# Expert loop of a two-layer encoder trunk: eight trips of one expert become four trips of two, and one selection matrix of 256 columns gathers the rows of both

## The reference

```
logits = (h @ w_router).astype(jnp.float32) + b_router.astype(jnp.float32)
top_val, top_idx = lax.top_k(logits, TOP_K_EXPERTS)
top_w = jax.nn.softmax(top_val, axis=-1)
gates = jnp.sum(jax.nn.one_hot(top_idx, N_EXPERTS, dtype=jnp.float32) * top_w[..., None], axis=-2)
for e in range(N_EXPERTS):
    out = out + gates[..., e:e + 1] * swiglu(h, w_gu[e], w_down[e])
```

## Time and profile before

| | us |
|---|---|
| median of three runs | 1984.95 |
| the profiled execution | 1984.88 |
| its span | 1983.1 |
| PE busy (share of the span) | 1940.6 (98%) |
| DVE busy | 1545.9 (78%) |
| ACT busy | 1278.7 (64%) |
| mean granted TensorE clock | 0.995 of full |
| HBM read | 510.53 MB |

### The profile page before, as it was taken

The page is one execution under the profiler, slowest core; times in us unless marked ns, Lnnn a source line. Parts: engine busy times, 40 slices in busy tenths (PEclk is TensorE's granted clock), DMA queues, the critical chain, the costliest instruction groups (busy, mean ns, idle before and its releaser), DMA issues.

```text
span 1983.1 us, 28233 instructions
## 1 busy us (share of the span) xinstructions
PE 1940.6 (98%) x9436; PEld 1610.3 (81%) x9436; DVE 1545.9 (78%) x1754; ACT 1278.7 (64%) x1698; POOL 58.2 (3%) x83
## 2 busy tenths in 40 slices
PE   8999999999999999999899999999999999999997
PEld 6887788888888887788788888888888888888886
DVE  4887665555456887664698998989989899898996
ACT  4647544544445647544577787777877778777785
POOL 1020000000000010001000000000000000000000
PEclk9999999999999999999999999999999999999998
DMA  8453554555554454553499999999999999999993
GB/s 269 137 189 109 194 206 139 169 192 198 182 191 132 128 173 149 193 197 110 148 362 352 354 377 346 353 350 352 379 354 347 348 351 380 349 352 350 355 375 149
DMA packets 178005, 512.52 MB, mean 258 GB/s; under 512 B 8225, under 2 KB 17377, under 8 KB 177938
## 3 DMA queue, kind: packets, MB, share of 16 engines
q1 hardware_dynamic: 175266, 502.47, 70.2%
q0 software_dynamic: 2544, 9.09, 1.5%
q10 hardware_dynamic: 128, 0.08, 0.0%
HBM read 510.53 MB, written 1.07 MB: 258 GB/s over the span
## 4 chain that ended last, share of the span: by engine, by line
PE 84%; DVE 7%; issue 4%; ACT 3%; POOL 1%; DMA 1%; DVEq 0%; SPq 0%; ACTq 0%; POOLq 0%
PE bank L867 14%; PE bank L862 14%; PE bank L863 14%; PE bank L1679 7%; PE bank L1685 7%; PE bank L1693 7%; PE bank L660 4%; PE bank L673 4%; PE bank L669 4%; DVE wlo L487 3%; PE bank L1706 2%; PE bank L812 2%; PE bank L906 1%; ACT whi L484 1%; PE bank L1977 1%
## 5 line engine op out<-in xcount | busy, mean ns | idle before, releaser
L487 DVE TENSOR_TENSOR wlo<-raw,whi 128x1024 fp32r<-128x1024 f32 (+3 forms) x958 | 1130.6, 1218 | 185.7 <-ACT whi L484 155.7
L484 ACT ACTIVATE whi<-raw 128x1024 fp32r<-128x1024 f32 (+3 forms) x958 | 995.2, 1057 | 281.7 <-PE bank L867 156.5
L862 PE MATMUL bank<-whi,xg_hi 128*128 128x512 f32 x896 | 351.8, 393 | 1.7 <-ACT whi L484 1.7
L863 PE MATMUL bank<-whi,xg_lo 128*128 128x512 f32 x896 | 348.9, 389 | 0.0
L867 PE MATMUL bank<-wlo,xg_hi 128*128 128x512 f32 x896 | 277.1, 390 | 3.1 <-DVE wlo L487 3.1
L867 PEld LDWEIGHTS bank<-wlo,xg_hi 128*128 128x128 f32 x896 | 167.4, 188 | 41.7 <-DVE wlo L487 7.1
L862 PEld LDWEIGHTS bank<-whi,xg_hi 128*128 128x128 f32 x896 | 168.2, 188 | 36.1 <-ACT whi L484 2.1
L863 PEld LDWEIGHTS bank<-whi,xg_lo 128*128 128x128 f32 x896 | 168.3, 188 | 34.0
L862 PE MATMUL bank<-whi,hidTw_hi 128*128 128x512 f32 x448 | 175.8, 392 | 0.0
L863 PE MATMUL bank<-whi,hidTw_lo 128*128 128x512 f32 x448 | 174.4, 389 | 0.0
L1679 PE MATMUL bank<-whi,hT_hi 128*128 128x512 f32 (+3 forms) x576 | 152.5, 388 | 6.0 <-ACT hT_hi L1375 5.1
(11 more groups left out here) (317 smaller groups left out, 2029.5 us busy)
## 6 DMA issues: line engine op xcount, KB each, us to landing
raw<-in_moe_w_gu SPq DMA_DIRECT2D x224, 1024.0 KB, 6.9
raw<-in_moe_w_down SPq DMA_DIRECT2D x112, 1024.0 KB, 7.3
raw<-in_w_in SPq DMA_DIRECT2D x34, 1024.0 KB, 5.1
raw<-in_ffn_w_gu SPq DMA_DIRECT2D x28, 1024.0 KB, 5.2
raw<-in_xa_wkv SPq DMA_DIRECT2D x16, 1024.0 KB, 5.0
raw<-in_ffn_w_down SPq DMA_DIRECT2D x14, 1024.0 KB, 4.9
raw<-in_w_branch SPq DMA_DIRECT2D x12, 1024.0 KB, 5.0
raw<-in_w_out SPq DMA_DIRECT2D x8, 1024.0 KB, 5.0
```

The costliest lines, as they stand in the source:

```text
L484: self.eng.activation(whi[:, ps, 0:size], src, ACT.Copy).then_inc(high_ready, mark(high_ready, "high", p))
L487: self.eng.tensor_tensor(wlo[:, ps, 0:size], src, whi[:, ps, 0:size].bitcast(F32), ALU.subtract).then_inc(low_ready, mark(low_ready, "low" ...
L862: pe.matmul(bank[b][:, :], hi[:, k], wh, start=first, stop=False)
L863: pe.matmul(bank[b][:, :], lo[:, k], wh, start=False, stop=False)
```

## The change

The loop has four trips of two experts. `find` fills `pick` with 256 columns, 128 for either expert; the gather for the next two experts stands in the second half of a trip, in two parts. `h` itself is kept split: ACT makes `h_hi`, DVE `h_lo`, both float32r, so the gather is a float32r product, with `pick` in float32r. It takes the high halves first and the low halves after. The body of a trip holds both experts' code, and the queues of ACT, DVE and SP have twice the length too. Core of the diff:

```diff
-            "experts": (1, segments[1][0], segments[1][1], E, 0),
+            "experts": (1, segments[1][0], segments[1][1], E // 2, 0),
...
-        def gather_pe(pe, g, which):
+        GATHER = ((1, 3), (0, 2))
+
+        def gather_pe(pe, g, which, part):
 
             pe.wait_ge(expert_step, at(g, "pick", which))
-            if which == "first":
-                pe.wait_ge(norm_ready, at(1, "ffn", "normed", 1))
-            for half in range(2):
-                b = GATHER[half]
+            for t in range(NT):
+                pe.wait_ge(high_copied, at("h_hi", t))
+            for b in GATHER[part]:
                 fill(pe, b, "dve")
-                for i in range(4):
-                    for t in range(NT):
-                        ins = pe.matmul(bank[b][:, i * P:(i + 1) * P], h[:, t, (4 * half + i) * P:(4 * half + i + 1) * P],
-                                        pick[:, t], start=t == 0, stop=t == NT - 1)
-                ins.then_inc(bank_full[b], mark(bank_full[b], g, "gather", which, half))
+            for low in range(2):
+                for t in range(NT):
+                    if low:
+                        pe.wait_ge(norm_ready, at("h_lo", t))
+                    for n_, b in enumerate(GATHER[part]):
+                        for i in range(2):
+                            k = 4 * part + 2 * n_ + i
+                            src = h_lo[:, t] if low else h_hi[t]
+                            ins = pe.matmul(bank[b][:, i * 2 * P:(i + 1) * 2 * P], src[:, k * P:(k + 1) * P], pick[:, t, :],
+                                            start=not low and t == 0 and i == 0, stop=bool(low) and t == NT - 1 and i == 1)
+                        if low and t == NT - 1:
+                            ins.then_inc(bank_full[b], mark(bank_full[b], g, "gather", which, part, n_))
...
             with tally.trips(pe, g, trips):
                 q = [0]
...
+                for hf in range(2):
+                    e = f"{g}.{hf}"
+                    mine = slice(hf * P, hf * P + P)
...
+                        if j == N - 1:
+                            if hf:
+                                gather_pe(pe, g, "next", 0)
+                            down(j - 1, last=2)
+                            turn_hidden(j)
+                            if hf:
+                                gather_pe(pe, g, "next", 1)
+                            down(j - 1, first=2)
...
                 for t in range(NT):
-                    dve.tensor_scalar(pick[:, t], iota, cur[:, t:t + 1], None, ALU.is_equal).then_inc(
-                        expert_step, mark(expert_step, g, "pick", which))
+                    for hf in range(2):
+                        dve.tensor_scalar(pick[:, t, hf * P:(hf + 1) * P], iota, cur[:, hf, t:t + 1], None, ALU.is_equal).then_inc(
+                            expert_step, mark(expert_step, g, "pick", which))
...
+                expert(f"{g}.0", gate_back, False)
+                expert(f"{g}.1", cur[:, 0, 2:4], True)
...
+        def split_h(dve, t):
+            dve.wait_ge(high_copied, at("h_hi", t))
+            dve.scalar_tensor_tensor(h_lo[:, t, :], h[:, t, :], rstd(1, "ffn", t), h_hi[t][:, :].bitcast(F32), ALU.mult,
+                                     ALU.subtract).then_inc(norm_ready, mark(norm_ready, "h_lo", t))
...
+                    act.wait_ge(rstd_ready, at(l, "ffn", "rstd"))
+                    high_of_h(0)
                     act.wait_ge(bank_full[0], at("router"))
                     act.activation(logits_T[:, :], bank[0][0:E, 0:S], ACT.Copy).then_inc(
                         act_freed[0], mark(act_freed[0], "logits_out"))
+                    high_of_h(1)
...
                     dve.wait_ge(rstd_ready, at(l, "ffn", "rstd"))
-                    for t in range(NT):
-                        dve.tensor_scalar(h[:, t, :], h[:, t, :], rstd(l, "ffn", t), None, ALU.mult).then_inc(
-                            norm_ready, mark(norm_ready, l, "ffn", "normed", t))
+                    split_h(dve, 0)
                 if l:
                     route(dve)
-                    mixer_dve(dve, sp_, "experts", lambda: route_again(dve))
+                    mixer_dve(dve, sp_, "experts", lambda: (split_h(dve, 1), route_again(dve)))
```

More of the change, by code:

```diff
@@ L824, in back_pe @@
+        def gathered_pe(pe, g, which):
+            for part in range(2):
+                for n_, b in enumerate(GATHER[part]):
+                    pe.wait_ge(dve_freed[b], at("lo", g, "gather", which, part, n_))
+        def back_pe(pe, e, which, t):
+            pe.wait_ge(dve_freed[4], at(e, "y", 0, which))
+            pe.wait_ge(dve_freed[5], at(e, "y", 1, which))
             for nb in range(2):
@@ L841, in mixer_pe @@
             l, u0, p0, trips, rnd = MIXERS[g]
-            gather_pe(pe, g, "first")
+            for part in range(2):
+                gather_pe(pe, g, "first", part)
             fill(pe, 4, "dve")
@@ L852, in mixer_pe @@
                 q = [0]
[L854 to L882, removed]
-                        else:
-                            parts = [(per * i + c, b0, per * i + c == 0, per * i + c == KD - 1) for c in range(per)]
-                        piece((xg_hi, xg_lo), parts, False)
-                    same(g, name, j)
@@ L888, in down @@
[L888 to L899, removed]
@@ L939, in mixer_act, with high_gathered, take_y @@
             l, u0, p0, trips, rnd = MIXERS[g]
[L941 to L947, removed]
+            def high_gathered(which, part):
+                for n_, b in enumerate(GATHER[part]):
+                    act.wait_ge(bank_full[b], at(g, "gather", which, part, n_))
+                    k = 4 * part + 2 * n_
+                    act.activation(xg_hi[:, k:k + 2], heads(bank[b][:, :], 2),
+                                   ACT.Copy).then_inc(high_copied, mark(high_copied, "hi", g, "gather", which, part, n_))
+            def take_y(e, which, full):
                 for nb in range(2):
@@ L950, in take_y @@
                     act.activation(y_hi[:, 512 * nb:512 * nb + 512], bank[4 + nb][:, :], ACT.Copy).then_inc(
-                        y_high, mark(y_high, g, "y high", nb, which))
-            high_gathered("first")
+                        y_high, mark(y_high, e, "y high", nb, which))
+            for part in range(2):
+                high_gathered("first", part)
             act.wait_ge(bank_full[4], at(g, "empty", 0))
@@ L1001, in mixer_dve, with find @@
+                expert(f"{g}.0", lambda step: previous(f"{g}.1", step), False)
+                expert(f"{g}.1", lambda step: at(f"{g}.0", step), True)
+            take_y(g, "last", [(bank_full[4], final(f"{g}.1", "out0")), (piece_used, final(f"{g}.1", "out1"))])
         def mixer_dve(dve, sp_, g, meanwhile=lambda: None):
             l, u0, p0, trips, rnd = MIXERS[g]
-            def find(which, row):
+            def find(which, rows):
                 if which == "first":
@@ L1008, in find @@
                 else:
[L1009 removed]
+                    dve.tensor_copy(gate_back[:, :], cur[:, 1, 2:4]).then_inc(expert_step, mark(expert_step, g, "gate back", which))
                 dve.wait_ge(expert_step, at(g, "gate back", which))
[L1011 removed]
+                dve.tensor_copy(cur[:, :, :], rows).then_inc(expert_step, mark(expert_step, g, "cur", which))
                 dve.wait_ge(expert_step, at(g, "cur", which))
@@ L1014, in find @@
                 for t in range(NT):
-                    dve.tensor_scalar(pick[:, t], iota, cur[:, t:t + 1], None, ALU.is_equal).then_inc(
-                        expert_step, mark(expert_step, g, "pick", which))
-            def low_gathered(which):
-                for half in range(2):
-                    dve.wait_ge(high_copied, at("hi", g, "gather", which, half))
-                    b = GATHER[half]
-                    dve.tensor_tensor(xg_lo[:, 4 * half:4 * half + 4], heads(bank[b][:, :], 4), xg_hi[:, 4 * half:4 * half + 4].bitcast(F32),
-                                      ALU.subtract).then_inc(dve_freed[b], mark(dve_freed[b], "lo", g, "gather", which, half))
@@ L1025, in take_y, with low_gathered @@
-            def take_y(which):
+                    for hf in range(2):
+                        dve.tensor_scalar(pick[:, t, hf * P:(hf + 1) * P], iota, cur[:, hf, t:t + 1], None, ALU.is_equal).then_inc(
+                            expert_step, mark(expert_step, g, "pick", which))
+            def low_gathered(which, part):
+                for n_, b in enumerate(GATHER[part]):
+                    dve.wait_ge(high_copied, at("hi", g, "gather", which, part, n_))
+                    k = 4 * part + 2 * n_
+                    dve.tensor_tensor(xg_lo[:, k:k + 2], heads(bank[b][:, :], 2), xg_hi[:, k:k + 2].bitcast(F32),
+                                      ALU.subtract).then_inc(dve_freed[b], mark(dve_freed[b], "lo", g, "gather", which, part, n_))
@@ L1040, in mixer_dve @@
-            find("first", tab[:, rnd, 0:1, :])
```

(26 more changed lines are left out.)

282 lines of the change are left out of this document (180 added, 102 removed).

## The result

The changed kernel takes 1993.14 us (median of five, 1991.42 to 1995.33) against 1984.95 us (1983.18 to 1985.75): a ratio of 1.0042, interval 1.0031 to 1.0053, so 8.2 us slower. The forecast was 1983.4. The profiled execution took 1995.33 us with a span of 1993.5.

What follows compares the result with a forecast made beforehand. The prediction took the expert loop to be bound by PE, with DVE next. Its terms, -13.3 - 0.6 + 1.0 + 7.2 + 4.2 = -1.5 us, gave 1983.4 us from 1984.88, range 1971.5 to 1989.5.

Steps and rivals of the forecast that it cites:

- Gathers: Expert loop: four float32r gathers of 3.81 us replace eight float32 ones of 3.57 us on PE; 13.3 us less.
- `find`: PE's wait behind DVE's `find` in the expert loop: four longer ones instead of eight; 0.6 us less.
- Ahead of the loop: Before the expert loop: splitting `h`, two more selections and a longer first gather add 1.0 us, bounds 0 and 2.
- so I take 2.4, between 1.9 and the full 3.4: PE's idle gap at each of three backward branches, the doubled body being fetched again; +7.2 us, bounds 0 and 10.1.
- The sequencer's net lead: At the loop's branch: 2.4 us ahead less about 0.9 of waits, hiding 1.5 of the extra 3.37 us.
- The clock: Half clock on PE behind the three branches: half of 2.8 us taken for each, +4.2 us, bounds 0 and 8.5.
- the clock falls at every branch: Rival at the edges between trips: full 3.4 us gaps and 2.8 us for each clock fall; 1990.6 us, chance 0.16.
- The first rival: The doubled loop body stays loaded, so PE's backward branches cost no refetch; 1972.0 us, chance 0.25.

Runs made afterwards that it cites:

- after_no_loop: The changed kernel with the four trips of its expert loop written out on PE, ACT, DVE and SP, so no branch goes back; 1969.72 us, ratio 0.9927.

## Why the prediction was wrong

**Gathers: right.** The last trip's two parts take 1.91 and 1.99 us, 3.90 against 3.81, 0.119 us for each matmul, as read from the earlier trace rows. From the loop's first matmul to its last piece's first, the trips written out take 974.34 us (976.86 to 1951.20) after the change and 988.13 (976.24 to 1964.37) before it: 13.8 less, against 13.9 forecast with `find`.

**`find`: right.** PE's wait behind it, against the earlier trace rows, four times instead of eight:

```profile
1126.74 0.39 PE L877 MATMUL bank<-whi,xg_lo 128*128 128x512 f32 x1
1127.88 0.73 PE L881 MATMUL bank<-wlo,xg_hi 128*128 128x512 f32 x2 [0.75 <-DVE wlo L489]
```

**Ahead of the loop: right for what it counted.** The loop's first matmul is 1.15 us later (978.30, before 977.15); forecast +1.0. Uncounted was the half clock from 978.31 to 981.72, 1.7 us, which the other kernels (above) show as a chance of this execution, not a cost of the change. The half-clock stretch ahead of it, which in both kernels covers the first gather, was not the last one this time.

**The step that failed: "so I take 2.4, between 1.9 and the full 3.4".** That the body would be fetched anew at each of three edges was right, and PE's branch does make the gap. The size was wrong, and beyond its upper bound: 15.1 us against 7.2, bound 10.1. I took the branch's length from a jump at 1973.0 us with no transfer beside it, and treated the load traffic as a small addition; it adds 2.5 us to 3.5, as the kernels with fewer loads show. The sequencer's net lead was also 1.0 us (6.08 less 5.09) and not 1.5: the branch came 1.6 us before PE fell idle, not 2.4, and 0.6 us passed between its end and the next matmul, not 0.9. The first part stays unexplained: in the old body doubled the branch came 2.6 us ahead, a net lead of 2.0.

**The clock: mis-sized with it.** Half of 2.8 was a chance of one in two, not a mechanism. Behind gaps of 5 us it fell three times of three, 7.2 us in total, and 1.7 at the start: 8.9 against 4.2. Only one gap of 2.5 us, with few loads, left it full. With gaps of the length that I had assumed the term would have been about right: 1.7 us for each of two falls, 3.4 in all. The rival "the clock falls at every branch" (1990.6) was nearest in mechanism and in time, and had been given 0.16.

**The sum in the profiled executions.** 1995.33 - 1984.88 = +10.45. Against the stretch before (977.15 to 1966.44, 989.29), the gathers and `find` bring -13.8, the loop's own arithmetic is -1.2 (989.29 - 988.13; seven edges become three), gaps +15.1, clock +8.9, start +1.15. That is +10.2, and 0.2 stay unassigned. The median of the runs is 2.2 lower than this execution. The dip at the loop's start, 1.7 us, would be most of that if the others lack it, but no profile of them is on record.

**The first rival, a body that stays loaded** (1972.0), is what after_no_loop reaches from the other side, 1969.72, by never jumping back.

## What to carry to other kernels

Before a loop's body grows, count PE's sequencer instructions in a trip, weight loads and matmuls each as one: here a body of 1687 had a branch of 0.2 us and no gap, and one of 1771 cost 6.8 us an edge. Price an instruction miss from a stretch with the transfers it will meet, not from a quiet one, and add the half clock behind the gap. Where a body is too large anyway, writing out all trips costs nothing here: straight code was fetched at the pace of its execution, and no idle time of PE in the loop ended by "issue".

## What was not expected of the hardware

- A taken branch to code no longer held costs PE 3.4 to 3.6 us with the loads' queue at 14.5%, 4.8 to 5.0 at 60%, and 5.9 to 6.1 at 94%. Other bodies that weren't held took 5.0 to 7.1 us beside the full loads.
- The step between held and not held lies between 1687 and 1771 PE instructions (1719 and 1803, if each float32 matmul is two), and past it all of the body is fetched again, not the excess.
- One gap of 2.4 to 2.6 us in a loop otherwise full left the clock full, two others of that length brought 3.41 us at half. Behind the 28 gaps of 3.17 to 4.99 us at the edges of all these kernels' trips it was 3.41 us 23 times and 6.83 five times (the shortest of these 4.00), behind the 12 of 5.00 us and more always 6.83.
